# Hybrid HGRN2 / RWKV-7 / mixture-of-experts layer: scans without a loop, an inverse grown by predicated copies, modulation inside the first projection

## The reference

```python
mod  = silu(c)     @ w_mod + b_mod          # six rows of 1024: sh1, sc1, g1, sh2, sc2, g2
modc = silu(c_ctx) @ w_mod + b_mod          # the same for the context
h, hc = layer_norm(x) * (1 + sc1) + sh1, layer_norm(ctx) * (1 + csc1) + csh1
p, pc = h @ w_in, hc @ w_in                 # q, i, zf, zb, g (HGRN2) and r, k, v, lora inputs (RWKV-7)
# context tokens only make the start states of the scans: no output is read from them
# HGRN2, 4 heads of 128, both directions:  s = exp(f) * s + k v',   o = q s
# RWKV-7, 8 heads of 64, both directions:
def step(s, inp):
    rt, wt, kt, vt, kkt, at = inp
    sa = einsum('nbhij,nbhj->nbhi', s, kkt)
    s = s * wt[..., None, :] - sa[..., :, None] * (kkt * at)[..., None, :] + vt[..., :, None] * kt[..., None, :]
    return s, einsum('nbhij,nbhj->nbhi', s, rt)
# then readout, out projection, norm, hierarchical top-1 group / top-2 expert layer, norm
```

## Time and profile before

| | us |
|---|---|
| median of 3 runs (lowest, highest) | 4801.01 (4797.78, 4803.33) |
| profiled execution, its own time | 4793.64 |
| its span, first to last instruction | 4792.0 |
| PE busy in the span | 4118.3 (86%) |
| DVE, POOL, ACT busy | 2245.3, 1458.4, 1140.0 |
| mean granted PE clock, share of full speed | 0.938 |

### The profile page before, as it was taken

How to read it: one execution, slowest core, us unless ns; L and a number is a source line. 1 busy time by engine, 2 the same in 40 slices (tenths; PEclk the granted TensorE clock), 3 DMA queues, 4 the chain that set the end, 5 groups by cost and what they waited for, 6 DMA issues and landing times. The chain is left out here.

```text
span 4792.0 us, 108835 instructions
## 1 busy us (share of the span) xinstructions
PE 4118.3 (86%) x40994; PEld 2767.1 (58%) x40994; DVE 2245.3 (47%) x3896; ACT 1140.0 (24%) x2810; POOL 1458.4 (30%) x1647
## 2 busy tenths in 40 slices
PE   2999979999996887888888886786899999998997
PEld 0777856766665777777787773443333333333333
DVE  1111146776764766666666656888111111111115
ACT  0100034444442333333333332321000000000000
POOL 0000001011113656565565643442322222212220
PEclk7999989999998999999999997887899999999998
DMA  9421146555554242423232326431967899999877
GB/s 289 180 71 56 47 126 213 185 196 199 192 184 145 78 132 71 130 74 117 85 117 86 110 62 198 138 131 58 351 254 300 357 381 377 384 395 403 344 276 294
DMA packets 330784, 933.02 MB, mean 195 GB/s; under 512 B 73488, under 2 KB 172176, under 8 KB 281008
## 3 DMA queue, kind: packets, MB, share of 16 engines
q1 hardware_dynamic: 276560, 779.01, 45.4%
q0 software_dynamic: 46944, 131.97, 7.5%
q10 hardware_dynamic: 6912, 16.78, 0.9%
HBM read 970.11 MB, written 209.17 MB: 246 GB/s over the span
## 5 line engine op out<-in xcount | busy, mean ns | idle before, releaser
L2535 PE MATMUL exp_gate_up<-exp_w_gate,exp_rows_and_rowsT 128*64 128x512 f32 x1664 | 743.1, 603 | 49.0 <-DMA exp_w_up<-in_moe_w_up_dram 47.9
L2535 PE MATMUL exp_gate_up<-exp_w_up,exp_rows_and_rowsT 128*64 128x512 f32 x1664 | 743.9, 604 | 0.0
L2535 PEld LDWEIGHTS exp_gate_up<-exp_w_gate,exp_rows_and_rowsT 128*64 128x64 f32 x1664 | 229.3, 139 | 533.9 <-issue 533.8
L738 PE MATMUL rwp_product<-rwp_hT,rwp_w_rw 128*128 128x256 f32 (+1 forms) x2016 | 443.1, 383 | 0.0
L2486 DVE TENSOR_TENSOR exp_hidden<-exp_hidden,exp_gate_up 64x512 f32<-64x512 f32 x104 | 71.9, 692 | 749.7 <-ACT exp_hidden L2467 749.7
L1574 POOL TENSOR_TENSOR rw_A_level<-rw_A_rho_beta,const_level_masks 128x512 f32<-128x512 f32 x216 | 308.9, 1440 | 358.1 <-DVE rw_A_rho_beta L1602 311.4
L738 PEld LDWEIGHTS rwp_product<-rwp_hT,rwp_w_rw 128*128 128x128 f32 (+1 forms) x2016 | 380.3, 189 | 61.0
L891 PE MATMUL hgp_product<-hgp_hT,const_w_hg 128*128 128x256 f32 x1728 | 393.7, 383 | 15.7 <-DMA hgp_hT<-s_hT 15.7
L2560 PE MATMUL exp_down<-exp_w_down,exp_hiddenT 128*64 128x512 f32 x1664 | 380.0, 598 | 1.2
L891 PEld LDWEIGHTS hgp_product<-hgp_hT,const_w_hg 128*128 128x128 f32 x1728 | 326.6, 192 | 70.4 <-DMA hgp_hT<-s_hT 16.1
L2467 ACT ACTIVATE exp_hidden<-exp_gate_up 64x512 f32<-64x512 f32 x104 | 61.3, 589 | 973.6 <-PE exp_gate_up L2535 973.6
(11 more groups left out here) (392 smaller groups left out, 7294.6 us busy)
## 6 DMA issues: line engine op xcount, KB each, us to landing
exp_w_gate<-in_moe_w_gate_dram SPq DMA_DIRECT2D x208, 1024.0 KB
exp_w_up<-in_moe_w_up_dram SPq DMA_DIRECT2D x208, 1024.0 KB
exp_w_down<-in_moe_w_down_dram SPq DMA_DIRECT2D x104, 2048.0 KB
s_rw_in<-prep_operands SPq DMA_DIRECT2D x72, 514.0 KB, 4.1
rw_operands<-s_rw_in SPq DMA_DIRECT2D x72, 514.0 KB, 6.9
hg_qkf<-s_hg_in SPq DMA_DIRECT2D x36, 768.0 KB, 8.5
rw_tokens<-s_rw_tm SPq DMA_DIRECT2D x144, 192.0 KB, 3.9
mod_w<-in_w_mod_dram SPq DMA_DIRECT2D x24, 1024.0 KB, 26.1
```

Of the source, the lines that this page charges most:

```text
L738: mm = nc.tensor.matmul(mp[o % 2][0:width, 0:GROUP], w_in[:, k, c0 - 5 * D_HG:c0 - 5 * D_HG + width], hT[b][:, k, :], start=(k == 0), stop ...
L2535: i = nc.tensor.matmul(pgu[u][q:q + BLK], xT[:, k, r * BLK:(r + 1) * BLK], w[r][:, k, :], start=(k == 0), stop=(k == KD - 1))
```

## The change

**Start.** The stage `modulation` is gone. A class `Modulation` is called from `rw_projection`. Part 0 of `w_mod` (shift and scale of the first norm) is loaded first, into the room of `w_hg`; its two rows are copied, transposed on PE and made into the columns `cols` by four DVE instructions, without a way through DRAM. Parts 1 and 2 are loaded over it and multiplied after `products(0)` and `products(1)`; their rows are stored by POOL. `w_hg` is loaded after part 2 is used.

**Context group.** What no output reads isn't made: in group 0 of `rw_projection` the four r tiles and the last lora tile (5 of 14 products), in group 0 of the next stage the four q and the two g outputs (DVE memsets in their place).

**Scans.** All 18 couples are written out. `RW_ORDER` is another, with the first chunk's chain between the Gram products. POOL's level masks are gone: `cross` multiplies by the whole A, and DVE copies under the level's mask (`copy_predicated`) into R, which ACT starts as the identity (one copy for each d). The decay of the state moves from DVE to POOL. The last couple's final state is left out, since nothing reads it.

```diff
...
-def modulation(nc, A, S, K):
...
+class Modulation:
...
+    def load_w(self, sp, b):
+        if b > 0:
+            sp.wait_ge(self.s["part_done"], b)
+        for k in range(KD):
+            sp.dma_start(self.w[:, k, :], self.A["w_mod"][0, k * P:(k + 1) * P, b * 2 * D:(b + 1) * 2 * D]).then_inc(self.got[k // 2], 16)
...
+    def pe(self, pe, b):
+        nc, s = self.nc, self.s
+        if b == 0:
+            pe.wait_ge(s["silu_done"], 1)
+        elif b == 1:
+            pe.wait_ge(s["part_copied"], 4)
+        else:
+            pe.wait_ge(s["rows_added"], 4)
+        for k in range(KD):
+            if k % 2 == 0:
+                pe.wait_ge(self.got[k // 2], 32 * (b + 1))
+            for j in range(4):
+                mm = nc.tensor.matmul(self.acc[32 * j:32 * j + 2, :], self.cs[:, k, :], self.w[:, k, j * 512:(j + 1) * 512],
+                                      start=(k == 0), stop=(k == KD - 1))
+        mm.then_inc(s["part_done"], 1)
...
+        dead = lambda g, o: isinstance(g, int) and g == 0 and (o < 4 or o == NO - 1)
...
+                mod.load_c(sp)
                 load_x(0, 0)
+                mod.load_w(sp, 0)
+                mod.load_rest(sp)
                 for b, (lo, hi) in enumerate(blocks):
                     if b == 1:
                         load_x(1, 1)
                     for k in range(KD):
                         sp.dma_start(w_in[:, k, lo - 5 * D_HG:hi - 5 * D_HG], A["w_in"][0, k * P:(k + 1) * P, lo:hi]).then_inc(w_loaded[b], 16)
                 load_x(2, 0)
+                mod.load_w(sp, 1)
+                mod.pads(sp)
+                mod.load_w(sp, 2)
+                load_x(3, 1)
+                load_x(4, 0)
+                sp.wait_ge(mod.s["part_done"], 3)
                 for k in range(KD):
                     sp.dma_start(K["w_hg"][:, k, :], A["w_in"][0, k * P:(k + 1) * P, 0:5 * D_HG]).then_inc(s["hg_w_loaded"], 16)
-                with sp.Fori(1, NG // 2) as i:
+                with sp.Fori(2, NG // 2) as i:
                     load_x(2 * i + 1, 1)
                     load_x(2 * i + 2, 0)
...
+                mod.dve_start(dve)
                 ahead(0, 0, 0, 0)
                 ahead(1, 1, 0, 1)
                 outputs(0, 0, 0)
+                mod.dve_rows(dve, 1)
                 ahead(2, 0, 1, 1)
                 outputs(1, 1, 0)
+                mod.dve_rows(dve, 2)
...
+                pe.wait_ge(mod.s["ident_ready"], 1)
                 turn(0, 0)
+                mod.pe(pe, 0)
+                mod.pe_turn(pe)
                 turn(1, 1)
                 products(0, 0)
+                mod.pe(pe, 1)
                 turn(2, 0)
                 products(1, 1)
+                mod.pe(pe, 2)
...
+def unused(g, kind):
+    return isinstance(g, int) and g == 0 and kind in "qg"
...
+            if unused(g, kind):
+                if kind == "q":
+                    pe.sem_inc(s["product_done"], 1)
+                continue
...
-RW_ORDER = ("gram0a gram0b rhs_a gram1a gram1b solve_a cross1 grow1 out_a cross2 grow2 state_a cross3 grow3 rhs_b "
-            "cross4 grow4 solve_b cross5 out_b grow5 state_b").split()
+RW_ORDER = ("gram0a rhs_a gram0b solve_a gram1a out_a gram1b state_a cross1 grow1 rhs_b cross2 grow2 solve_b cross3 grow3 "
+            "out_b cross4 grow4 state_b cross5 grow5").split()
...
-            pe.wait_ge(s["level_ready"], 6 * m + l + 1)
             pe.sem_inc(self.turns, 1)
             for v, j, q in both_heads:
-                i = nc.tensor.matmul(self.pa[d][q, v, j, :], self.al[d][l % 2][q, v, j, :], self.rT[d][q, v, j, :], start=True, stop=True)
+                i = nc.tensor.matmul(self.pa[d][q, v, j, :], self.ar[u][d][q, v, j, 0, :], self.rT[d][q, v, j, :], start=True, stop=True)
             i.then_inc(s["x_psum"], 1)
...
+        def ident(d):
+            s = self.s[d]
+            wait(act, s["u_psum"], 2 * m - 2)
+            nc.scalar.activation(self.r[u][d][:].rearrange("p v j t -> p (v j) t"), self.K["idc"][:].unsqueeze(1).broadcast_to([P, 2 * NPAIR, RW_C]),
+                                 ACT.Copy).then_inc(s["ident_ready"], 1)
...
+        def decay(d, v):
+            s, c = self.s[d], 2 * m - 2 + v
+            pool.wait_ge(s["s_order"], c + 1)
+            nc.gpsimd.tensor_tensor(self.st[d][:], self.st[d][:], self.ch[v][d][:, 2 * XW:HEAD].unsqueeze(2).broadcast_to([P, NPAIR, RW_C]),
+                                    ALU.mult).then_inc(s["s_ready"], 1)
...
+        for v, x in enumerate("ab"):
             c = 2 * m - 2 + v
+            if with_output(m, 1):
+                steps += [(rw_time(f"state_{x}", d, 2.6), lambda d=d, v=v: decay(d, v)) for d in range(2)]
+                if with_output(c, RW_CTX):
+                    steps.append((rw_time(f"state_{x}", 1, 2.7), lambda c=c: self.store(pool, c)))
...
-            r = self.r[u][d]
+            heads = lambda t: t.rearrange("p v j t -> p (v j) t")
+            level = K["lvc"][:, d, l, :].bitcast(U32).unsqueeze(1).broadcast_to([P, 2 * NPAIR, RW_C])
             if l == 0:
-                dve.wait_ge(s["level_ready"], 6 * m + 1)
-                wait(dve, s["u_psum"], 2 * m - 2)
-                V.tensor_tensor(r[:].rearrange("p v j t -> p (v j) t"), self.al[d][0][:].rearrange("p v j t -> p (v j) t"),
-                                K["idc"][:].unsqueeze(1).broadcast_to([P, 2 * NPAIR, RW_C]), ALU.add).then_inc(s["grown"], 1)
+                dve.wait_ge(s["masked"], 4 * m + 2)
+                dve.wait_ge(s["ident_ready"], m + 1)
+                new = self.ar[u][d][:].rearrange("p v j x t -> p (v j) x t")[:, :, 0, :]
             else:
                 dve.wait_ge(s["rd_psum"], 5 * m + l)
                 dve.wait_ge(s["r_ready"], 6 * m + l)
-                V.tensor_tensor(flat(r[:]), flat(r[:]), flat(self.pa[d][:]), ALU.add).then_inc(s["grown" if l < 5 else "r_ready"], 1)
+                new = heads(self.pa[d][:])
+            dve.sem_inc(self.dve_turns, 1)
+            V.copy_predicated(heads(self.r[u][d][:]), level, new).then_inc(s["grown" if l < 5 else "r_ready"], 1)
...
-            dve.wait_ge(s["s_order"], c + 1)
-            V.tensor_tensor(self.st[d][:], self.st[d][:], self.ch[v][d][:, 2 * XW:HEAD].unsqueeze(2).broadcast_to([P, NPAIR, RW_C]),
-                            ALU.mult).then_inc(s["s_ready"], 1)
...
-        steps += [("gram1a", 2.7, lambda d: inverse(d, 0)), ("gram1b", 2.8, lambda d: turned(d, 0))]
+        steps += [("solve_a", 1.6, lambda d: inverse(d, 0)), ("gram1a", 2.2, lambda d: turned(d, 0))]
...
-HG_GAPS = [rw_gap(x) for x in RW_ORDER[RW_ORDER.index("cross1"):]]
-HG_AT = ([(0.0, 0.0), (0.015, 0.01), (HG_SUM, rw_time("gram0b", 1, 1.7)), (HG_ENDS, rw_time("gram0b", 1, 1.8)), (0.09, rw_time("gram1b", 1, 0.0))]
+HG_GAPS = [rw_gap(x) for x in RW_ORDER[RW_ORDER.index("gram1b"):]]
+HG_AT = ([(0.0, 0.0), (0.015, 0.01), (HG_SUM, rw_time("gram0a", 1, 1.7)), (HG_SUM + 0.01, rw_time("gram0b", 1, 1.7)),
+          (HG_ENDS, rw_time("gram0b", 1, 1.8)), (0.09, rw_time("out_a", 0, 0.0))]
          + [(hg_time(t), g) for t, g in enumerate(HG_GAPS)] + [(HG_OUT, 1.0), (2.0, 2.1)])
...
-    peel(eng, HG_STEPS // 2, turn)
+    for g in range(HG_STEPS // 2):
+        turn(g)
...
-STAGES = [modulation, rw_projection, hg_projection_and_prep, scans, readout, experts, combine]
+STAGES = [rw_projection, hg_projection_and_prep, scans, readout, experts, combine]
```

346 lines of the change are left out of this document (197 added, 149 removed).

## The result

The changed kernel takes 4523.24 us in the median (4512.54 to 4528.33), against 4799.4 us before; the ratio is 0.9428, with a 95% interval of 0.9400 to 0.9457.

A forecast was written before the change was run, and what follows sets the result against it. PE was taken to bound projection and scans, with waits and issue gaps, and the w_mod load to set modulation. Gains of 48 + 17 + 149 = 214 us gave 4587 us from a median of 4799.4, range 4540 to 4668.

The forecast's parts named there:

- Part 1: The start: modulation moved into the first projection lets products(2) start near 188 us instead of 235.91, 48 us gained.
- Part 2: Context group of the second projection: without q and g outputs the window falls from 88.7 to 72 us, 17 us gained.
- Part 3: The scans' loop: six back edges, each with idle time and a slow Gram product, go by writing out; 50 us gained.
- Part 4: Order and predicated copies in the scans: most PE waits go, steady couple 72.5 us; 149 us with part 3's 50.
- two thirds: Share of PE's 37.1 us wait for HGRN2's scaled q and k claimed gone, as POOL falls to about 35 us a couple.
- (C): Rival for the scans: all waits go, a couple near 69 us, 60 us more gain, 4527 us; chance 0.12.
- (A): Rival for the scans: gaps stay in other places, couple about 76.5 us, 4655 us; chance 0.22 together with (E).
- (B): Rival for the start: not overlapped, SP queue delays x behind weights, gain 20 instead of 48, 4615 us; chance 0.06.
- (D): Rival for the scans: slower than before, rhs waits for POOL's late decays, 4801 us passed, say 4830; chance 0.02.
- (E): Rival for the loop: writing out does nothing, idle time being fetching; 50 us less gain, 4637; chance 0.22 with (A).

The follow-up runs named there:

- pool_load: The changed kernel with POOL making its twelve level masks a couple again, into tiles nobody reads: 0.9635 of before, 99 us over the changed kernel.
- pool_memset: The changed kernel with a POOL memset of 128x1500, which reads nothing, in place of each level mask: 0.9543 of before, 55 us over the changed kernel.
- loop: The changed kernel with the loop over seven rounds of two couples put back: 0.9510 of before, 39 us over the changed kernel.
- unrolled: The kernel before with nothing changed but that all 18 couples are written out: 0.9846 of before.
- decay_dve: The changed kernel with the state's decay multiplication back on DVE, behind its addition: 0.9435 of before, 3 us over the changed kernel.

## Why the prediction missed

**Part 1** (48 us forecast, 55 measured): right step by step; the constants landed at 33 and the first product stood at 64.4 for 68, products(2) at 181.7 for 188.

**Part 2** (17, measured nothing clear of noise in two pairs of kernels): the step that failed was to take the group's own length for the stage's. The group did become 10.6 us shorter, inside my bounds, by a limit that I called DVE at 80% (60.0 in 72 is 83%). That PE then idles 8 us and works more slowly behind it, and that the next four groups give back 11.9 us, I had not weighed.

**Part 3** (50, measured 74 to 80 in the kernel before, 28 to 39 in the changed one): the idle time at the back edges was read rightly, though its rows add up to 7.9 us and not 8.3, 47 for 50 (3.10 + 2.37 + 2.4). But the odd couples also became shorter, in part as four of nine 5 us stalls went. I had counted a loop's cost only where its idle time stands. That is 30 us of what the scans gained above the 149, if the loop is taken out first.

**Part 4** (99 of its own, 127 measured) is the other term that was mis-sized, by 28 us; together the two took the time out of the range. Of 7.2 us of waits for data in a couple I left 3.3 "in all"; the waits named in the profile after are 1.2 a couple. Issue was 3.1 where I said 3.8, some of it waits as well, and PE's own work 64.3 for 65.4. Measured are 68.1 us a couple for 72.5, over 14 couples some 60 us: the surplus of the scans, 207 for 149. The 3.3 doesn't follow from my own rows: a third of the 37.1 us for the scaled q and k is 0.7 a couple, the small waits 0.5 and the copies 0.5, so 1.7; the other 1.6 had no reason. And the "two thirds" was a guess: the 50.2 us at the scaled scores fell to 11.2, and `pool_load` and `pool_memset` bring them back to 74 to 76 by POOL's load alone. What I charged for the copies, 0.5 us a couple, is the 0.05 us that each is longer, times ten. Couple 17, less 9.7 and 1, should have given 10.7 and not 12. I said that the 5.17 us row agrees with the rule of the shared read port, held for an instruction: the two inputs in SBUF agree, the length doesn't, as no POOL instruction beside it took over 1.3 us and the stall spans six of them.

Of the signs, equal couples, no slow Gram products at their start, no 5 us row and POOL at 34 to 35 us came; couples of 72 to 73 us and a second projection 17 us shorter didn't.

**The rivals.** (C), all waits go and a couple takes near 69 us, 4527, is what happened. It had a chance of 0.12, and its time lay outside my range, since I had cut the range at half of it. That 4523 is so near to its 4527 is in part luck: the 7 us more at the start and the 17 us missing in the second projection are no part of (C). The weakness was there in the text: I gave the waits one row each, named the edit that removed each, and still left 3.3. (A), (B), (D) and (E) did not come; (E), that writing out does nothing, falls with `loop` and `unrolled`.

## What to carry to other kernels

Where two engines share a read path and one of them has a queue that the critical engine waits for, take work off it even if nobody waits for that work: masks that stood in no one's way cost 99 us in 1205. When every wait on a path has an edit that removes it, forecast them gone and put the doubt in the range, not in the value. And work removed at a stage's start is a gain only when the stage's end moves: the idle time that it opens can make the work behind it slower. Read the end, not the group.

## What the runs showed of the hardware

- A DVE multiplication of 128x256 takes 0.43 us, and 5.17 us beside a POOL that goes from one SBUF-reading instruction to the next; in `decay_dve`, beside a POOL busy half of the time, no row is over 0.92 us.
- DVE's differences of 128x512 take 0.87, 1.00 and 1.42 us beside a POOL with 34 us of work in a couple, with memsets added, and with masks added.
- The stall of 5.17 us spans six POOL instructions in a row and ends 0.3 us behind the last (2160.11 and 2159.81).
- Gaps that the profile names issue can be waits: 1.29 and 1.93 us in `unrolled` end 0.19 and 0.10 us behind a POOL instruction, in one couple as in the next.
- The same loop, with two couples in a round, cost 74 us in the kernel before and 39 in the changed one.
- After 7.96 us without work PE ran the next group at a granted clock of 0.94, 89.0 us for work of 85.5 at 0.98.
